# Narrower moving operands for the value product and the router product of a one-core hybrid attention and mixture-of-experts layer

## Chip, core and metric

The program runs on one NeuronCore of a Trainium2 chip. The metric is the device time of one execution in microseconds (us). Its engines are TensorE (PE in the rows, with its weight loads listed apart as PEld), VectorE (DVE), ScalarE (ACT), GpSimd (POOL) and SyncE (SP), which here issues most of the DMA transfers. On TensorE a product has a stationary operand, which is loaded by an instruction LDWEIGHTS, and a moving operand, whose columns are then streamed by MATMUL.

## What is computed

One layer over 1024 prompt tokens and 8 x 16 sample tokens. Of the reference, the change touches two products, the last line of the sparse attention and the two router products of the mixture of experts:

```python
    p = jax.nn.softmax(logits, axis=-1).astype(v.dtype)
    return jnp.einsum('bqhn,bqnhd->bqhd', p, v_sel)            # 8 heads of 64 columns
...
    g_logits = (x @ w_router_group + b_router_group).astype(jnp.float32)      # 4 columns
...
    e_logits = (x @ w_router_expert + b_router_expert).astype(jnp.float32)    # 16 columns
```

All inputs are float32. Around these lie a combined input projection, an indexer that picks 256 keys for each query, a recurrent branch, an output projection with a layer norm, and 16 experts.

## The kernel before

The kernel is written engine by engine; the order on each engine is the order of its code, and semaphores tie the engines together. Two kinds of product occur. `mm3` (lines 492 to 494) splits float32 operands into a high and a low part of type fp32r and makes three products. `mm` of two plain float32 tiles becomes two pairs of LDWEIGHTS and MATMUL in the trace: two passes over the same columns. `tr` is a product with the identity that transposes; it is one pair.

**Attention over the prompt.** Tokens lie in 8 query tiles of 128, each with 8 heads. PE runs a loop over i = 0 to 66, with query tile t = i // 8 and head h = i % 8. An iteration issues, in this order, the logits of head i (line 1054: stationary the padded queries, moving 128(t+1) key columns), the value product of head i - 3 (line 1066: stationary a block of 128 x 128 of the transposed probabilities `PT`, moving columns of `V`, t+1 blocks, so 2(t+1) passes) and the transposes of the probabilities of head i - 2 (line 1075). DVE takes the row maximum (line 1769), ACT the exponential (lines 1399 and 1400), and the two take turns, by odd and even head, to copy the transposed probabilities to `PT` (ACT line 1407, DVE line 1777). The value product of a head waits for this copy, the transposes wait for the exponential, and the logits wait for the row maximum of the head two before.

Before the change the value product streams the 128 columns of a pair of heads and leaves 128 columns in PSUM for each head; the 64 that belong to the head are read from there:

```python
v.tensor_tensor(ON[...], PS[:, 6 + hf, :].rearrange("p (k r c) -> p k r c", k=2, r=2)[:, :, r, HD * r:HD * r + HD], ...)
```

The whole loop has 288 such products (8 heads x 36 blocks), which are 576 passes.

**Router.** There are 9 token tiles. After the layer norm `turn_x1(t)` transposes a tile (line 1150, 8 pairs), ACT copies it to `X1T` (line 1547), and `router(t)` multiplies it with the router weights `RLG` (line 1161, 8 products, 16 passes). `RLG` has 128 columns, of which 20 are loaded by DMA; POOL clears it first (line 854), and SP waits for that before it loads the weights (line 697). The first routers are issued between the last products of the output projection, router(t - 4) after its token tile t and before turn_x1(t - 3); the last ones come behind it, each waiting for ACT's copy. DVE adds the bias (line 1911) and goes on to the choice of experts.

Three other places are used as rows below. Line 909 at the start transposes the input tokens (128 columns each). Line 936 is a single float32 product with a stationary block of 128 x 128 and 8 moving columns. Line 914 is a run of 8 transposes of 40 rows: 128 stationary columns, 40 moving ones.

Of the kernel before, what the change touches and what calls it, by code (L numbers as in the profile page):

```python
# [11 lines left out]
KB = D // 128  # L12
# [4 lines left out]
H, HD = 8, 64  # L17
# [42 lines left out]
def build(nc, I, O):  # L60
# [3 lines left out]
    def sb(name, shape, at, dt=f32):  # L64
        return nc.alloc_sbuf_tensor_at(name, shape, dt, offset=at)
# [50 lines left out]
    R2 = XLo + 36864  # L116
# [11 lines left out]
    V = sb("v", [128, TT, 512], R3)  # L128
# [39 lines left out]
    PT = sb("p_T", [128, 2, 1024], R6 + 18432 + 12288)  # L168
# [42 lines left out]
    WC = 256  # L211
    NWC = D // WC
    X1T = sb("x1_T", [128, 3, KB, 128], R2)
    RLG = sb("router", [128, KB, 128], R2 + 12288)
    LNP = sb("ln_params", [128, 4, D], M2)
    C0 = M2 + 16384

# [38 lines left out]
    PS = nc.alloc_psum_tensor("psum", [128, 8, 512], f32)  # L256
# [72 lines left out]
    s_block_products = sem("block_products")  # L329
# [45 lines left out]
    s_zero = sem("zero")  # L375
# [60 lines left out]
    blocks = []  # L436
# [129 lines left out]
    with nc.Block() as block:  # L566
# [3 lines left out]
        def _(sp):  # L570
# [123 lines left out]
                sp.dma_start(YACC[:, t, :], x_rows(t)).then_inc(s_xres[1], 16)  # L694
            sp.wait_ge(s_block_merged, 2 * KB)
            sp.dma_start(BEFORE[:, :], I["c_before"]).then_inc(s_lnp, 16)
            sp.wait_ge(s_zero, 2)
            with nc.allow_non_contiguous_dma(reason="router weights have short rows"):
                for c_, name, w in ((0, "w_router_group", 4), (4, "w_router_expert", 16)):
                    sp.dma_start(RLG[:, :, c_:c_ + w], I[name].rearrange("(k p) n -> p k n", p=128)).then_inc(s_lnp, 16)  # L700
# [12 lines left out]
                sp.dma_start(WD[e][:, :, :], WD_D[e]).then_inc(s_down_loaded[e], 16)  # L713
            sp.wait_ge(s_slot, 1)
            with sp.If(overflowing(sp)):
                sp.wait_ge(s_zero, 3)
                with sp.Fori(0, E) as e:
                    for j in range(MT_MAX - 1):
                        for h in range(2):
                            sp.dma_start(XS_N[bass.ds(e, 1), j][:, :, h, :].rearrange("o p d -> (o p) d"),  # L720
                                         XG[:, 0, 0, :]).then_inc(s_of, 16)
# [48 lines left out]
        def _(pool):  # L770
            g = nc.gpsimd
# [78 lines left out]
            pool.wait_ge(s_smp_out_turned, BATCH_S)  # L850
            for p_ in range(BA_0, NPIECE):
                split_piece(p_)
            pool.wait_ge(s_block_products, 3 * len(blocks))
            g.memset(RLG[:, :, :], 0.0).then_inc(s_zero, 1)
            pool.wait_ge(s_w_out_products, 1)
            for c in range(1, NWC):
                for q in range(2):
# [41 lines left out]
        def _(pe):  # L899
            mm, tr = nc.tensor.matmul, nc.tensor.transpose  # L900
            pe.wait_ge(s_misc, 16)
            for t in range(TT):
                for hf in range(2):
# [4 lines left out]
                    for k in range(4):  # L908
                        last = tr(PS[:, i % 4, 128 * k:128 * k + 128],
                                  XIN[:, t % 3, 128 * (4 * hf + k):128 * (4 * hf + k) + 128], IDENT)  # L910
                    last.then_inc(s_x_transposed, 1)
            pe.wait_ge(s_const, 16 * 10)
            for k in range(KB):
                last = tr(PS[:, 4, NV * k:NV * k + NV], VIN[0:NV, 128 * k:128 * k + 128], IDENT[0:NV, 0:NV])
# [45 lines left out]
            for c, (name, c0, w) in enumerate(CHUNKS):  # L960
                for t in range(TT):
# [19 lines left out]
                    if name == "kw":  # L981
                        last = tr(PS[:, gi % 4, 0:KW], KWT[:, ts], IDENT[0:KW, 0:KW])
# [62 lines left out]
            for i in range(TP * H + 3):  # L1045
                if i < TP * H:
                    t, h = divmod(i, H)
                    hp, n = h // 2, 128 * (t + 1)
                    if h == 0:
                        pe.wait_ge(s_queries_padded, t + 1)  # L1050
                    wait(pe, s_max_done, i - 1)
                    for k0 in range(0, n, 512):
                        m = min(512, n - k0)
                        last = mm(PS[:, 2 * (i % 2) + k0 // 512, 0:m], QZ[t % 2][:, h, :], KT[:, hp, k0:k0 + m],  # L1054
                                  start=True, stop=True)
                    last.then_inc(s_logits, 1)
                if i >= 3:
                    a = i - 3
                    t, h = divmod(a, H)
                    if h == 0 and t >= 1:  # L1060
                        turn_out(t - 1)
                    if h == H // 2:
                        wait(pe, s_attn_lo, t)
                    pe.wait_ge(s_p_T_stored[a % 2], a // 2 + 1)
                    for k in range(t + 1):
                        last = mm(PS[:, 6 + h // 4, 128 * (h % 4):128 * (h % 4) + 128], PT[:, a % 2, 128 * k:128 * k + 128],  # L1066
                                  V[:, k, 128 * (h // 2):128 * (h // 2) + 128], start=k == 0, stop=k == t)
                    last.then_inc(s_values_added, 1)
                if 2 <= i < TP * H + 2:
                    a = i - 2  # L1070
                    t = a // H
                    pe.wait_ge(s_exp_done, a + 1)
                    wait(pe, s_p_T_stored[(a - 1) % 2], (a + 1) // 2)
                    for k in range(t + 1):
                        last = tr(PS[:, 4 + k // 4, 128 * (k % 4):128 * (k % 4) + 128],  # L1075
                                  P[:, a % 3, 128 * k:128 * k + 128], IDENT)
                    last.then_inc(s_p_turned, 1)
# [75 lines left out]
            def router(t):  # L1153

                pe.wait_ge(s_x1t, 2 * t + 2)
                wait(pe, s_logits_ready, t - 1)
                if t == 0:
                    pe.wait_ge(s_states_rows, 2)
                    pe.wait_ge(s_lnp, 16 * 7)
                for k in range(KB):  # L1160
                    last = mm(PS[:, 6 + t % 2, 0:128], X1T[:, t % 3, k, :], RLG[:, k, :], start=k == 0, stop=k == KB - 1)
                last.then_inc(s_logit_products, 1)

            for c in range(NWC):
# [864 lines left out]
```

## Time and profile before

| | |
|---|---|
| median of 3 runs | 1838.76 us (1838.23 to 1840.95) |
| profiled execution, span | 1838.4 us, 0.36 us below the median |
| PE busy | 1607.0 us (87%), 9886 pairs of load and product |
| DVE, ACT, POOL busy | 825.6, 537.5, 441.6 us |
| chain that ended last | PE 66%, DVE 22% |

The span runs from the first to the last instruction of the profiled execution, and the table's shares are shares of it. Nothing beyond the span is listed for that execution, so its own time is taken as the span. A matmul's duration includes the time in which its last columns run through the array; the next one starts before that, so the distance between two starts, not the duration, is what a product costs in a row of products.

### The profile page before, as it was taken

To read this page: it belongs to the slowest core of one execution; us is meant where nothing else is said; L and a number is where in the kernel's file an instruction comes from. 1 tells how busy PE (TensorE), PEld (TensorE's weight loads), DVE (VectorE), ACT (ScalarE), POOL (GpSimd) and SP (SyncE) were. 2 spreads that over 40 slices of the span, in tenths; PEclk is the share of its full clock that TensorE was granted. 3 is DMA by queue.
4 is the path that set the end of the run, shared out by engine and by line. 5 is a ranking of instruction groups with operands and counts; after the bars stand their busy time and mean duration, and the time that the engine had idled before them with its cause. 6 is when DMAs were issued, how large, how long until landed. Compare 5 with 4: busy or idle time off the path is not lost.

```text
span 1838.4 us, 24783 instructions
## 1 busy us (share of the span) xinstructions
PE 1607.0 (87%) x9886; PEld 1409.3 (77%) x9886; DVE 825.6 (45%) x1555; ACT 537.5 (29%) x1056; POOL 441.6 (24%) x482
## 2 busy tenths in 40 slices
PE   6988899999589988899999989999993499999920
PEld 5944699999567776799899889999993377777710
DVE  4048399999944443224455541114264011211117
ACT  4256222111155433204656530003111121111025
POOL 2700297422100000133343332332201200000045
PEclk8989999999899999999999999999997699999965
DMA  5100111222550007431111111116005687877645
GB/s 172 33 7 1 52 36 59 63 91 83 158 167 1 24 1 252 154 113 38 47 32 46 44 29 47 41 41 226 27 1 191 212 260 229 261 252 233 195 133 193
DMA packets 135785, 195.16 MB, mean 106 GB/s; under 512 B 14644, under 2 KB 88884, under 8 KB 135680
## 3 DMA queue, kind: packets, MB, share of 16 engines
q1 hardware_dynamic: 130496, 174.83, 30.2%
q0 software_dynamic: 5184, 18.88, 3.0%
q8 instruction: 72, 1.18, 0.3%
q14 instruction: 33, 0.27, 0.0%
HBM read 144.48 MB, written 49.20 MB: 105 GB/s over the span
## 4 chain that ended last, share of the span: by engine, by line
PE 66%; DVE 22%; DMA 3%; POOL 3%; ACT 3%; issue 2%; SPq 0%; POOLq 0%; DVEq 0%; ACTq 0%
PE psum L492 11%; PE psum L493 11%; PE psum L494 11%; PE psum L1209 9%; PE psum L1230 6%; DVE compare_out L1731 5%; DVE psum L1731 5%; PE psum L1066 4%; PE psum L1054 3%; PE psum L1028 2%; PE psum L1075 2%; PE psum L932 2%; DVE scores L1692 1%; PE psum L1201 1%; PE psum L1126 1%
## 5 line engine op out<-in xcount | busy, mean ns | idle before, releaser
L492 PE MATMUL psum<-x_hi,ring_hi 128*128 128x384 f32 x768 | 259.2, 337 | 0.5 <-ACT v L1366 0.5
L493 PE MATMUL psum<-x_hi,ring_lo 128*128 128x384 f32 x768 | 256.7, 334 | 0.0
L494 PE MATMUL psum<-x_lo,ring_hi 128*128 128x384 f32 x768 | 256.7, 334 | 0.0
L822 POOL CAST ring_hi<-ring_raw 128x512 fp32r<-128x512 f32 x88 | 65.0, 738 | 566.8 <-PE psum L494 394.8
L1209 PEld LDWEIGHTS psum<-expert_rows_T,w_gate_up 128*128 128x128 f32 x1024 | 169.1, 192 | 8.5 <-issue 8.5
L492 PE MATMUL psum<-w_hi,x_hi 128*128 128x256 f32 x576 | 169.3, 294 | 5.0 <-DVE channel_vectors L1637 3.7
L1209 PE MATMUL psum<-expert_rows_T,w_gate_up 128*128 128x192 f32 x1024 | 171.0, 329 | 0.7 <-ACT expert_rows_T L1562 0.7
L493 PE MATMUL psum<-w_hi,x_lo 128*128 128x256 f32 x576 | 164.7, 286 | 0.0
L494 PE MATMUL psum<-w_lo,x_hi 128*128 128x256 f32 x576 | 164.5, 286 | 0.0
L492 PEld LDWEIGHTS psum<-x_hi,ring_hi 128*128 128x128 f32 x768 | 144.2, 188 | 1.7 <-ACT v L1366 0.7
L493 PEld LDWEIGHTS psum<-x_hi,ring_lo 128*128 128x128 f32 x768 | 144.2, 188 | 1.1
L494 PEld LDWEIGHTS psum<-x_lo,ring_hi 128*128 128x128 f32 x768 | 144.2, 188 | 0.0
L823 POOL TENSOR_TENSOR ring_lo<-ring_raw,ring_hi 128x512 fp32r<-128x512 f32 x88 | 129.3, 1469 | 7.0
L492 PEld LDWEIGHTS psum<-w_hi,x_hi 128*128 128x128 f32 x576 | 112.2, 195 | 5.3 <-issue 3.8
L1230 PE MATMUL psum<-w_down,expert_hidden 128*96 128x512 f32 x256 | 112.6, 593 | 0.8 <-issue 0.8
L1731 DVE TENSOR_SCALAR_CACHE_REDUCE compare_out<-scores,candidate_bits 128x640 bf16<-128x640 f32 (+2 forms) x128 | 112.1, 876 | 1.1
L493 PEld LDWEIGHTS psum<-w_hi,x_lo 128*128 128x128 f32 x576 | 112.4, 195 | 0.0
L494 PEld LDWEIGHTS psum<-w_lo,x_hi 128*128 128x128 f32 x576 | 112.2, 195 | 0.0
L883 POOL DMA_INDIRECT gathered_expert_out<-y_by_expert,slot x18 | 24.1, 1341 | 333.1 <-issue 333.1
L1956 DVE TENSOR_TENSOR expert_hidden<-psum,expert_silu 128x384 f32<-128x384 f32 x16 | 8.9, 558 | 198.0 <-PE psum L1209 198.0
L1731 DVE TENSOR_SCALAR_CACHE_REDUCE psum<-scores,candidate_bits 128x512 f32<-128x512 f32 (+2 forms) x96 | 97.6, 1016 | 0.0
L1066 PEld LDWEIGHTS psum<-v,p_T 128*128 128x128 f32 x576 | 71.3, 194 | 29.4 <-DVE p_T L1777 12.8
(322 smaller groups left out, 3200.4 us busy)
## 6 DMA issues: line engine op xcount, KB each, us to landing
w_gate_up<-in_w_gate_up SPq DMA_DIRECT2D x16, 2048.0 KB, 8.9
ring_raw<-in_w_in SPq DMA_DIRECT2D x64, 256.0 KB, 3.0
w_down<-in_w_down SPq DMA_DIRECT2D x16, 1024.0 KB, 6.3
x_by_expert<-zeros SPq DMA_DIRECT2D x32, 384.0 KB, 5.2
expert_rows<-x_by_expert SPq DMA_DIRECT2D x16, 768.0 KB, 11.0
y_by_expert<-expert_out SPq DMA_DIRECT2D x16, 768.0 KB, 7.4
w_raw<-in_w_in SPq DMA_DIRECT2D x16, 512.0 KB, 4.5
k_cache<-in_cache_k SPq DMA_DIRECT2D x8, 1024.0 KB, 8.1
```

Of the source, the lines that this page charges most:

```text
L492: nc.tensor.matmul(out, ah, bh, start=first, stop=False)
L493: nc.tensor.matmul(out, al, bh, start=False, stop=False)
L494: return nc.tensor.matmul(out, ah, bl, start=False, stop=last)
L822: link(g.tensor_copy(RHI[:, p_ % 2, :, :], RRAW[:, p_ % 2, :, :]))
L823: g.tensor_tensor(RLO[:, p_ % 2, :, :], RRAW[:, p_ % 2, :, :], RHI[:, p_ % 2, :, :].bitcast(f32), ALU.subtract).then_inc(s_piece_split, 1)
L932: mm(PS[:, 4 + d % 4, 0:n], QIT[:, h // 2, 128 * t:128 * t + 128], (KIZ if h % 2 else KIT)[:, k0:k0 + n], start=True, stop=True).then_inc( ...
L1028: mm(PS[:, 6 + j % 2, 0:RC], WRG[:, gt, :], XC[:, RC * c:RC * c + RC], start=True, stop=True).then_inc(s_lru_gate_products, 1)
L1054: last = mm(PS[:, 2 * (i % 2) + k0 // 512, 0:m], QZ[t % 2][:, h, :], KT[:, hp, k0:k0 + m], start=True, stop=True)
L1066: last = mm(PS[:, 6 + h // 4, 128 * (h % 4):128 * (h % 4) + 128], PT[:, a % 2, 128 * k:128 * k + 128], V[:, k, 128 * (h // 2):128 * (h // ...
L1209: last = mm(PS[:, bank + m // 2, MS * (m % 2):MS * (m % 2) + MS], wg[:, k, 128 * m:128 * m + 128], xgt[:, k, :], start=k == 0, stop=k == K ...
L1230: last = mm(PS[0:MR, 6 + j % 2, :], HE[:, par, k, MR * h:MR * h + MR], WD[par][:, k, 512 * nn:512 * nn + 512], start=k == 0, stop=k == 1)
L1731: v.tensor_scalar(out[:, 0:n], SC[:, o_:o_ + n], CAND[:, j:j + 1].bitcast(f32), c0_, ALU.is_ge, ALU.add, accum_out=CNT[:, j:j + 1]).then_i ...
```

## The change

`V` is indexed by the head's own 64 columns, which are written to the place in PSUM that DVE already reads; `RLG` has 20 columns; the clearing of `RLG` and SP's wait for it are gone, and the count of the one later wait on that semaphore is one lower.

```diff
-    RLG = sb("router", [128, KB, 128], R2 + 12288)
+    RLG = sb("router", [128, KB, 20], R2 + 12288)
...
             sp.dma_start(BEFORE[:, :], I["c_before"]).then_inc(s_lnp, 16)
-            sp.wait_ge(s_zero, 2)
             with nc.allow_non_contiguous_dma(reason="router weights have short rows"):
...
-                sp.wait_ge(s_zero, 3)
+                sp.wait_ge(s_zero, 2)
...
-            pool.wait_ge(s_block_products, 3 * len(blocks))
-            g.memset(RLG[:, :, :], 0.0).then_inc(s_zero, 1)
...
                     for k in range(t + 1):
-                        last = mm(PS[:, 6 + h // 4, 128 * (h % 4):128 * (h % 4) + 128], PT[:, a % 2, 128 * k:128 * k + 128],
-                                  V[:, k, 128 * (h // 2):128 * (h // 2) + 128], start=k == 0, stop=k == t)
+                        o0 = 128 * (h % 4) + HD * (h % 2)
+                        last = mm(PS[:, 6 + h // 4, o0:o0 + HD], PT[:, a % 2, 128 * k:128 * k + 128],
+                                  V[:, k, HD * h:HD * h + HD], start=k == 0, stop=k == t)
...
-                    last = mm(PS[:, 6 + t % 2, 0:128], X1T[:, t % 3, k, :], RLG[:, k, :], start=k == 0, stop=k == KB - 1)
+                    last = mm(PS[:, 6 + t % 2, 0:20], X1T[:, t % 3, k, :], RLG[:, k, :], start=k == 0, stop=k == KB - 1)
```

No instruction changes its place on any engine: PE has as many rows as before. PE in the second query tile of the attention, before (a float32 product stands in one row here, for both of its passes; the last number is the output's columns):

```order
L1066 MATMUL psum<-v,p_T 128x128 [waits p_T_stored_0]
L1066 MATMUL psum<-v,p_T 128x128
L1075 MATMUL psum<-misc,p 128x128 [waits p_T_stored_0,exp_done]
L1075 MATMUL psum<-misc,p 128x128
L1054 MATMUL psum<-k_T,q_padded_111 128x256 [waits max_done]
```

The same place on PE after the change, where the file is three lines shorter above it:

```order
L1064 MATMUL psum<-v,p_T 128x64 [waits p_T_stored_0]
L1064 MATMUL psum<-v,p_T 128x64
L1073 MATMUL psum<-misc,p 128x128 [waits p_T_stored_0,exp_done]
L1073 MATMUL psum<-misc,p 128x128
L1051 MATMUL psum<-k_T,q_padded_111 128x256 [waits max_done]
```

Only the output's columns differ; the waits and the neighbours are the same.

## Rows read from the trace of the kernel before

**Rows 1.** The page: span, and the chain that ended last, by engine and line.

```profile
span 1838.4 us, 24783 instructions
...
PE 66%; DVE 22%; DMA 3%; POOL 3%; ACT 3%; issue 2%; SPq 0%; POOLq 0%; DVEq 0%; ACTq 0%
PE psum L492 11%; PE psum L493 11%; PE psum L494 11%; PE psum L1209 9%; PE psum L1230 6%; DVE compare_out L1731 5%; DVE psum L1731 5%; PE psum L1066 4%; PE psum L1054 3%; PE psum L1028 2%; PE psum L1075 2%; PE psum L932 2%; DVE scores L1692 1%; PE psum L1201 1%; PE psum L1126 1%
```

**Rows 2.** Busy us (instructions) of PE, PEld, DVE, ACT, POOL, then PEclk, DMA share, GB/s.

```profile
518.00:597.00 79.00, 74.86 (x464) 55.45 (x463) 40.08 (x113) 42.78 (x122) 4.88 (x8) 1.00 0.18 52
597.00:677.00 80.00, 79.15 (x513) 62.25 (x511) 37.66 (x64) 37.46 (x75) 1.22 (x2) 1.00 0.04 14
```

**Rows 3.** Timeline, 660 to 667 us: start, length of the run, instruction, count.

```profile
660.20 1.95 PE L1066 MATMUL psum<-v,p_T 128*128 128x128 f32 x16
...
664.58 1.95 PE L1066 MATMUL psum<-v,p_T 128*128 128x128 f32 x16
664.58 1.75 PEld L1066 LDWEIGHTS psum<-v,p_T 128*128 128x128 f32 x15 [0.24 <-issue]
666.36 0.93 PE L1075 MATMUL psum<-misc,p 128*128 128x128 f32 x7
```

**Rows 4.** Timeline around lines 936 and 914.

```profile
181.09 0.30 PEld L936 LDWEIGHTS psum<-misc,wi_spread 128*128 128x128 f32 x2 [3.72 <-issue]
181.20 0.19 PEld L936 LDWEIGHTS psum<-misc,wi_spread 128*128 128x128 f32 x1
181.12 0.36 PE L936 MATMUL psum<-misc,wi_spread 128*128 128x8 f32 x2 [2.92 <-DVE wi_spread L1698]
27.20 0.57 PEld L914 LDWEIGHTS psum<-misc,vectors_in 40*128 40x128 f32 x8 [0.17 <-issue]
```

**Rows 5.** Groups by line and shape: count, busy us, mean ns of one.

```profile
L1066 PE MATMUL psum<-v,p_T 128*128 128x128 f32 x576 | 79.9, 284 | 8.3 <-ACT p_T L1407 5.3 <-DVE p_T L1777 2.6
L1054 PE MATMUL psum<-k_T,q_padded 128*128 128x512 f32 x96 | 47.8, 593 | 0.0
```

**Rows 6.** Who PE waited for, 518 to 597 us, then 504 to 518 us.

```profile
PE psum L1066 <- ACT p_T L1407: 3.0, 8, 0.7
...
PE psum L1054 <- DVE row_max L1769: 18.1, 1, 18.1
```

**Rows 7.** The last routers: timeline, and busy time of that stretch.

```profile
1389.81 2.05 PE L1161 MATMUL psum<-router,x_T 128*128 128x128 f32 x16 [0.74 <-ACT x_T L1547]
1393.47 2.05 PE L1161 MATMUL psum<-router,x_T 128*128 128x128 f32 x16 [0.74 <-ACT x_T L1547]
...
1385.00:1399.00 14.00, 10.61 (x88) 9.93 (x88) 4.10 (x9) 4.90 (x8) 0.00 (x0) 1.00 1.04 397
```

**Rows 8.** The same columns by stretch (second row: line 909 alone); then a timeline.

```profile
16.20:26.40 10.20, 5.81 (x26) 5.41 (x27) 4.35 (x7) 4.49 (x8) 0.00 (x0) 0.50 0.70 249
16.20:26.40 10.20, 5.81 (x26) 5.41 (x27) 0.50 0.70 249
26.40:29.80 3.40, 1.49 (x16) 1.20 (x14) 3.14 (x5) 1.29 (x3) 0.00 (x0) 0.99 0.00 0
504.50:514.50 10.00, 8.17 (x29) 6.61 (x30) 2.46 (x15) 6.92 (x28) 0.89 (x2) 0.50 0.99 289
514.50:527.00 12.50, 10.04 (x61) 7.07 (x61) 6.32 (x26) 7.44 (x29) 1.24 (x3) 1.00 0.95 272
1402.00:1449.00 47.00, 1.56 (x6) 1.46 (x6) 9.34 (x42) 0.21 (x1) 17.36 (x18) 0.50 0.60 224
...
510.25 0.42 PE L1054 MATMUL psum<-k_T,q_padded 128*128 128x128 f32 x1
511.41 0.64 PE L1054 MATMUL psum<-k_T,q_padded 128*128 128x128 f32 x2
```

**Rows 9.** The clearing on POOL, and SP's load of the router weights.

```profile
1262.82 0.95 POOL L854 MEMSET router<- 128x1024 f32 x1 [10.42 <-PE psum L494]
1269.13 0.43 SPq L700 DMA_DIRECT2D router<-in_w_router_group  x1
```

## Prediction

> **What bounds the kernel now.** I read the page first. The span is 1838.4 us, and the chain that ended last lies on PE for 66% of it, of which line 1066, the value product, holds 4% [rows 1]: some 70 us in which work can be saved, if the product gets shorter. Then the attention by stretch: from 597 us on (query tiles 5 to 7) PE is busy for 79.15 of 80.00 us, so there each nanosecond of PE counts; from 518 to 597 us (tiles 1 to 4) it is busy for 74.86 of 79.00, and DVE and ACT for half of the time [rows 2]. In those tiles the value product still waits now and then for ACT's copy of the probabilities (3.0 us in 8 waits), and in tile 0 PE waits for the row maximum (18.1 us in one wait) [rows 6].
>
> So the question is what a value product costs, load and stream. In a row of 16 passes the starts of 16 products span 1.95 us less one duration; the mean duration is 0.284 us [rows 3, 5], so a pass takes (1.95 - 0.28) / 15 = 0.111 us. The 15 loads tell the same: 1.75 us less one load of 0.19, over 14, is 0.111 us [rows 3, 4].
>
> What would the stream alone need? The duration grows from 284 ns at 128 columns to 593 at 512 [rows 5], that is 309 / 384 = 0.80 ns a column, 0.10 us for 128 columns and 0.05 for 64. What would the load alone need? Line 936 shows it: stationary 128 x 128 as here, but only 8 moving columns. Its first load starts at 181.09, its second at 181.20 [rows 4]. With almost nothing to stream, the next pass still comes 0.11 us later. Loads of float32 blocks of 128 columns follow each other at 0.11 us, whatever is streamed between.
>
> **The change, part by part.**
>
> *Value product, within a run.* 576 passes, each from 0.10 us of streaming to 0.05. By line 936 the load of 0.11 us takes the place of the stream, so a pass stays at 0.11 us: 0. The bounds: nothing, and 4 ns a pass (0.111 down to 0.107, the lower edge of the rounded 0.11), on the 512 passes that are followed by another of their run, 2.0 us. I take nothing.
>
> *Value product, at the end of a run.* The last pass of a run is followed by a transposing product of line 1075, whose load is shorter: the eight loads of line 914, also with 128 stationary columns, span 0.57 us, at most 0.07 us apiece, and since that includes all of the last load, I take 0.06 [rows 4]. Today the last pass streams 0.11 us before the transposes can stream; then it needs 0.05, and the short load 0.06. That saves 0.11 - 0.06 = 0.05 us in each of the 64 runs, one per head. In tiles 5 to 7 all of it counts: 24 x 0.05 = 1.2 us. In tiles 1 to 4 the heads are copied in turn by ACT and DVE, and the copy that waits behind an exponential or a row maximum hides part; I take half, 32 x 0.05 / 2 = 0.8 us (bounds 0 and 1.6). In tile 0 PE waits for the row maximum anyway: 0 (at most 8 x 0.05 = 0.4). Together 2.0 us, between 1.2 and 3.2.
>
> *Router.* The same, nine runs of 16 passes: 16 products in 2.05 us, less a first load and one duration, is again 0.11 a pass [rows 7]. Of 20 columns the stream is 0.02 us, the load still 0.11. After eight of the runs come the transposes of line 1150, 8 x 0.05 = 0.4 us; the last one's result comes 108 x 0.8 ns = 0.09 us earlier. All are in line: the last routers wait for ACT's copy [rows 7], which waits for the transposes of line 1150, which stand behind the router before on PE. Together 0.5 us, at most another 135 x 4 ns = 0.5 us.
>
> *Clearing and wait.* The 0.95 us on POOL end at 1263.77 us, SP issues the router weights at 1269.13 [rows 9], 5.4 us later: SP was held by its earlier transfers, not by the clearing. The transfers keep their number of pieces. If SP came to that place before POOL, the wait would have cost up to 0.95 us, and its removal would give that back; the late routers come 120 us later [rows 7], so the price is 0 either way.
>
> *Readers.* DVE reads the same 64 columns of PSUM as before. Nothing is added on another engine.
>
> Sum: 2.0 + 0.5 = 2.5 us off 1838.4, 1835.9 us. The median of the runs is 0.36 us above the profiled execution, so I forecast 1836.3.
>
> The Trainium skill's page "TensorE: Matmul & The Clock Gate" has rules for both answers. Its section on the back-to-back gap gives N / 2.4 + 2.5 ns for an isolated warm product, by which 64 columns fewer would give an estimated 27 ns for each of 576 passes, 15 us in all. Its section on LDWEIGHTS says that a load takes about P / 1.2 ns for P columns whatever else is in it, an estimate of 107 ns for 128, and by that rule the change would give almost nothing. The rows of line 936 side with the second.
>
> **The rivals.**
>
> *The stream sets the pace after all* (a load is fetched further ahead in a long run than line 936 with its two passes can show). Then a pass falls to about 0.055 us. Tiles 5 to 7 have 336 passes, 18.8 us; tiles 1 to 4 have 224, of which half counts, 6.3 us; the router's 144 passes fall from 0.11 to some 0.03, 12 us. Together 37 us, 1801 us. Against it: the loads of line 1066 do not run ahead of their products; fifteen of them take 0.111 us each [rows 3].
>
> *The upper bound of every term.* All 64 ends of runs (3.2 us), 4 ns on each pass (2.0 and 0.5), and the router's 0.5: 6.2 us, 1832.2, as a median 1832.6.
>
> *The clock.* The change takes columns from PE and leaves its pace. The granted clock shows what that can do: at the start of the attention it stays at 0.50 (1.2 GHz) for 10 us in which PE is busy for 8.17, and goes to 1.00 (2.4 GHz) only then; behind the routers it is at 0.50 for 47 us in which PE is busy for 1.56 [rows 8]. If the last routers, with 20 columns in place of 128, no longer look busy, the clock falls there and not behind them. At the lower clock two passes of 128 columns are 0.64 - 0.42 = 0.22 us apart [rows 8], twice as far. A round of router and transposes, 3.66 us from 1389.81 to 1393.47 [rows 7], would be longer by 16 x 0.11 and 8 x 0.11 us (a transpose, too, costs 0.11 at the higher clock, (0.93 - 0.28) / 6 in [rows 3]), 2.6 us. One round outweighs the gain; a fall at about 1388 us, behind the first late router, costs two rounds, a last router (1.8) and a set of transposes (0.9), 7.9 us: 1838.4 - 2.5 + 7.9 = 1843.8, as a median 1844.2. The time is longer than before by more than 0.2% once 2.4 rounds are hit. A later rise at the start of the attention is the same mechanism: each head of tile 1 (4 passes of value, 2 transposes, 2 passes of 256 columns) would cost up to 4 x 0.11 + 2 x 0.11 + 2 x 0.21 = 1.1 us more. For it: the stretch of the last routers keeps 10.61 busy us of 14.00 [rows 7] only as long as a pass that streams little counts. Against it: the transposes stay, and between 16.2 and 26.4 us PE ran nothing but the 26 transposes of line 909, and the clock rose from 0.50 to 0.99 behind them [rows 8]; and at the attention the runs of logits stay.
>
> If transposes did not count for the clock, the fall would be all but certain, since beside them the late routers stream almost nothing. The Trainium skill's page "TensorE: Matmul & The Clock Gate" says in its part on transposes that they do not count as busy in the same way. The trace disagrees: the rise to 0.99 at 26.4 us had only transposes before it.
>
> *No effect at all* (the ends of runs hidden too): 1838.8; it lies 2.5 us from the forecast and inside its own range.
>
> **How the numbers follow.** A measurement of this kernel tells about 0.2% (3.7 us) from no change, so faster means below 1835.1, slower above 1842.4. The forecast, loads that set the pace and a clock as before, with its own range 1834 to 1839: 0.63, of which 0.06 is below 1835.1. The upper bounds, 1832.5 to 1834.5: 0.12. The stream: 0.05. The clock: 0.20, between 1837 and 1845, 0.12 of it above 1842.4. Faster 0.06 + 0.12 + 0.05 = 0.23, slower 0.12, same 0.65. The range 1832.5 to 1842.5 leaves out the stream (0.05) and the worse half of the clock (0.12).
>
> **What would show it.** In the profile after, line 1066's counterpart: runs of 16 loads still 0.11 us apart while the duration of a product falls from 284 to about 230 ns; the first transposing product 0.06 us behind the last value product; 4.38 us per head in tile 7 (660.20 to 664.58, [rows 3]) become 4.33. The router's rounds 3.61 in place of 3.66. PEclk 1.00 until the routers end, and its rise in the attention within a few us of 10 us behind its start. The forecast is wrong if the loads follow each other faster than 0.10 us, or if the clock falls before 1395 us.

## The result, and the profile after

The changed kernel took 1851.71 us (median of 4 runs, 1846.45 to 1854.21), the kernel before 1839.64 us (4 runs): ratio 1.0062, 95% interval 1.0046 to 1.0078. It is slower by 8 to 14 us, where 2.5 us less was forecast. The profiled execution of the changed kernel took 1851.48 us and has a span of 1849.7 us, so 1.8 us lie outside a span; the comparisons below are of spans and of starts within them.

The page of the changed kernel, its span and the granted clock in 40 slices:

```profile
span 1849.7 us, 24775 instructions
...
PEclk8989899999799998999999999999995699999965
```

The chain that ended last is as in [rows 1], on PE for 66%, with the value product (now line 1064) at 3% in place of 4%. One slice of the clock row stands out: the 31st (1387 to 1434 us) shows 5. To find the 11.3 us, take the start of the same instruction in both traces at the borders of the stages. PE's timeline of the kernel before, then of the changed kernel (the rows are the first logits, the last value product, the first value product of the sample tokens, the first two routers and the last one, the experts' first transposes):

```profile
485.53 0.71 PE L1054 MATMUL psum<-k_T,q_padded 128*128 128x128 f32 x4 [0.58 <-ACT sigmoid_out L1389]
685.75 2.05 PE L1066 MATMUL psum<-v,p_T 128*128 128x128 f32 x16 [1.32 <-DVE p_T L1777]
707.04 1.07 PE L1126 MATMUL psum<-v_cache,p_sample_T 128*32 128x128 f32 x10
1359.60 2.05 PE L1161 MATMUL psum<-router,x_T 128*128 128x128 f32 x16 [0.72 <-ACT x_T L1547]
1365.24 1.95 PE L1161 MATMUL psum<-router,x_T 128*128 128x128 f32 x16
1397.14 2.05 PE L1161 MATMUL psum<-router,x_T 128*128 128x128 f32 x16 [0.74 <-ACT x_T L1547]
1449.06 3.06 PE L1201 MATMUL psum<-misc,expert_rows 96*128 96x96 f32 x16 [37.67 <-DMA expert_rows<-x_by_expert]
```

```profile
486.12 0.71 PE L1051 MATMUL psum<-k_T,q_padded 128*128 128x128 f32 x4 [0.58 <-ACT sigmoid_out L1387]
684.38 2.00 PE L1064 MATMUL psum<-v,p_T 128*128 128x64 f32 x16 [1.31 <-DVE p_T L1775]
708.45 1.07 PE L1124 MATMUL psum<-v_cache,p_sample_T 128*32 128x128 f32 x10
1360.98 2.24 PE L1159 MATMUL psum<-router,x_T 128*128 128x20 f32 x16 [0.72 <-ACT x_T L1545]
1368.16 1.86 PE L1159 MATMUL psum<-router,x_T 128*128 128x20 f32 x16
1394.22 3.60 PE L1159 MATMUL psum<-router,x_T 128*128 128x20 f32 x16 [0.69 <-ACT x_T L1545]
1400.28 3.60 PE L1159 MATMUL psum<-router,x_T 128*128 128x20 f32 x16 [0.69 <-ACT x_T L1545]
1406.35 3.60 PE L1159 MATMUL psum<-router,x_T 128*128 128x20 f32 x16 [0.69 <-ACT x_T L1545]
1460.01 3.05 PE L1199 MATMUL psum<-misc,expert_rows 96*128 96x96 f32 x16 [37.85 <-DMA expert_rows<-x_by_expert]
```

| stage, from start to start | before | after | difference |
|---|---|---|---|
| span's start to first logits | 485.53 | 486.12 | +0.59 |
| first logits to last value product | 200.22 | 198.26 | -1.96 |
| from there to the sample tokens' first value product | 21.29 | 24.07 | +2.78 |
| from there to first router | 652.56 | 652.53 | -0.03 |
| first router to last router | 37.54 | 45.37 | +7.83 |
| last router to the experts' transposes | 51.92 | 53.66 | +1.74 |
| from there to the span's end | 389.34 | 389.69 | +0.35 |

The attention gave what was forecast, 2.0 us. From the first value product of a tile to that of the next, tiles 1 to 4 are 0.83 us shorter and tiles 5 to 7 0.93. The other 0.19 lie in tile 0 and are not shown to be the change's: tile 0 took 11.85 us before, 11.66 after and 11.27 in run 2 below, whose value product is that of before and whose clock rose at 510 us in place of 514.5.

The rest was lost behind the attention, above all in the routers and what follows them. But each column of the table is one execution, and not every difference in it comes back in another. The late routers' does: from router 5 (counted from 0) to the experts' transposes it is 62.88 us before, 71.05 after and 70.89 in run 2, which has the narrow router too. The first router's does not: its start to the second's is 5.64 us before and 7.18 after, and 5.59 in run 2 with the same 20 columns. Nor does that of the stage behind the attention: beside 21.29 before and 24.07 after stand 23.53, 23.59 and 23.70 us in runs 2, 6 and 9, whose value product is that of before, and 21.47 in run 1, which has the narrow one. So some 4 us of the 11.3 are not shown to come from the change.

The same columns as [rows 2], for the changed kernel:

```profile
597.00:677.00 80.00, 78.68 (x515) 61.57 (x514) 38.06 (x64) 36.98 (x75) 1.22 (x2) 1.00 0.05 14
687.00:700.00 13.00, 10.24 (x45) 7.58 (x50) 3.99 (x8) 2.98 (x5) 0.00 (x0) 0.50 0.77 268
1385.00:1389.80 4.80, 3.26 (x30) 3.05 (x29) 4.66 (x9) 1.38 (x3) 0.00 (x0) 1.00 0.77 230
1389.80:1406.00 16.20, 14.49 (x66) 13.29 (x65) 2.17 (x6) 3.28 (x6) 0.00 (x0) 0.50 0.84 321
```

Read the granted clock, the seventh figure. Behind the attention it is at 0.50 (1.2 GHz) from 687 us on, where the kernel before fell at 695.4. In the late routers it falls at 1389.8 and stays at 0.50, although PE is busy for 14.49 of 16.20 us; before, the whole stretch ran at 1.00 [rows 7]. Ahead of the fall the busy times don't differ: PE is busy for 3.26 of the 4.80 us up to 1389.8, and before for 3.30 of the 4.80 us at the same place (1382.22 to 1387.02), both at 1.00. At 0.50 a router takes 3.60 us in place of 2.05, and a round, 1394.22 to 1400.28 and on to 1406.35, takes 6.06 in place of 3.66.

That the loads' pace itself did not change is seen in tile 7, PE's timeline of the changed kernel where the clock is at 1.00, with a piece of the loads' timeline:

```profile
659.12 1.89 PE L1064 MATMUL psum<-v,p_T 128*128 128x64 f32 x16
660.85 1.04 PE L1073 MATMUL psum<-misc,p 128*128 128x128 f32 x8
661.73 1.88 PE L1051 MATMUL psum<-k_T,q_padded 128*128 128x512 f32 x4
663.45 1.89 PE L1064 MATMUL psum<-v,p_T 128*128 128x64 f32 x16
...
663.45 0.64 PEld L1064 LDWEIGHTS psum<-v,p_T 128*128 128x128 f32 x5 [0.23 <-issue]
```

Five loads in 0.64 us, less one of 0.19, are still (0.64 - 0.19) / 4 = 0.11 us apart. The run of 16 is 1.89 long in place of 1.95 [rows 3], the transposes follow at 1.73, that is 0.06 behind the last pass's start (15 x 0.111 = 1.67), and a head takes 663.45 - 659.12 = 4.33 us in place of 4.38.

### The profile page after: what moved, and what is told of

Its sections match the earlier page's. It is cut to its first block, busy times and chain, and to the rows that moved or that the text cites. A ratio compares the mean times of both kernels' runs of the same rounds, so it can differ in the third digit from the quotient of the medians.

```text
span 1849.7 us, 24775 instructions
## 1 busy us (share of the span) xinstructions
PE 1617.7 (87%) x9879; PEld 1418.6 (77%) x9886; DVE 824.4 (45%) x1555; ACT 537.9 (29%) x1056; POOL 440.4 (24%) x481
## 4 chain that ended last, share of the span: by engine, by line
PE 66%; DVE 22%; DMA 3%; POOL 3%; ACT 3%; issue 2%; SPq 0%; POOLq 0%; DVEq 0%; ACTq 0%
PE psum L492 11%; PE psum L493 11%; PE psum L494 11%; PE psum L1207 9%; PE psum L1228 6%; DVE compare_out L1729 5%; DVE psum L1729 5%; PE psum L1064 3%; PE psum L1051 3%; PE psum L1025 2%; PE psum L929 2%; PE psum L1073 2%; PE psum L1199 1%; PE psum L1124 1%; DVE scores L1690 1%
```

## The experiments

The theory after the result: the loads set the pace of both products, and what was lost was lost by the granted clock, because PE streams fewer columns there and not because it is busy for less time. The rivals are named at each run. A profile shows one execution, and they differ ahead of the edits too: the attention's first value product starts at 507.84 us before and 508.42 after, but at 500.85, 504.83 and 503.89 in runs 3, 4 and 5, where PE waits less for the first row maximum (11.85 us in run 5, 18.08 before). So spans are compared by stage. Runs 1 to 4 were compared with the kernel before at 1838.65 us (30 executions), runs 5 to 8 at 1839.48 (34).

**1. The value product alone** (the diff's value part on the kernel before).

> Only the value product is narrow; the router keeps 128 columns, its clearing and its wait. Theory (fewer streamed columns let the clock fall): 2.0 us gained in the attention, about 2 lost again behind it because the clock falls at about 687 us as in the changed kernel; at the router PEclk stays 1.00 until about 1400. Time within 1.5 us of the kernel before. Rival (the clock falls at the router for another reason, such as an earlier attention): the late routers run at 0.50 here too, 8 us longer than before.

Measured: 1838.19 us (12 runs), ratio 1.0004 (0.9985 to 1.0022). First logits to last value product: 483.69 to 681.96, 198.27 us, the same 1.95 us less than before. The clock stayed at 1.00 in all routers and fell at 684.7 us. So this part alone is not what made the kernel slower; nor does its 2 us show in the median. That 2 us would be lost again behind the attention did not come out of the profile, although the clock fell there as expected. The last value product and the first value product of the sample tokens, in this run and then in run 2, which has 128 columns there:

```profile
681.96 2.00 PE L1067 MATMUL psum<-v,p_T 128*128 128x64 f32 x16 [1.32 <-DVE p_T L1778]
703.43 1.07 PE L1127 MATMUL psum<-v_cache,p_sample_T 128*32 128x128 f32 x10
...
682.65 2.05 PE L1063 MATMUL psum<-v,p_T 128*128 128x128 f32 x16 [1.31 <-DVE p_T L1774]
706.18 1.07 PE L1123 MATMUL psum<-v_cache,p_sample_T 128*32 128x128 f32 x10
```

That is 21.47 us here, with the fall at 684.7, and 23.53 in run 2, with the fall at 691.2.

**2. The router alone** (the changed kernel with the value product of before).

> Only the router is narrow (and its clearing and wait are gone); the value product keeps 128 columns. Theory (fewer streamed columns): the attention and the clock behind it are as before (1.00 until about 695 us), the late routers run at 0.50: 8 to 10 us slower than the kernel before. Rival (the router's columns are not the cause): within 1 us of the kernel before.

Measured: 1848.93 us (7 runs), ratio 1.0046 (1.0028 to 1.0065). Its late routers by stretch:

```profile
1387.50:1403.00 15.50, 14.13 (x65) 12.97 (x64) 2.00 (x6) 2.98 (x5) 0.00 (x0) 0.50 0.87 330
```

The last two routers in PE's timeline of this run:

```profile
1397.67 3.60 PE L1158 MATMUL psum<-router,x_T 128*128 128x20 f32 x16 [0.69 <-ACT x_T L1544]
1403.74 3.60 PE L1158 MATMUL psum<-router,x_T 128*128 128x20 f32 x16 [0.69 <-ACT x_T L1544]
```

Rounds of 6.07 us at 0.50, as in the changed kernel. The router's part of the change is enough, and most of the loss comes from it. It is the 108 columns fewer together with the clearing and the wait that are gone; run 8 lacks these two as well and keeps its clock, so their absence alone does not lower it. At the first router the clock held here.

**3. The changed kernel with one added product ahead of the first router and of each of routers 5 to 8.** The added product's result is not used:

```diff
+            def fill(done):
+                pe.wait_ge(s_mix_added, done)
+                mm(PS[:, 0, 0:256], IDENT, MISC[:, 0:256], start=True, stop=True)
...
             for t in range(TT - 3, TT):
+                fill(TT * NWC - 3)
                 router(t - 1)
                 turn_x1(t)
+            fill(TT * NWC - 3)
             router(TT - 1)
```

> The changed kernel with work added: one product of the identity with 256 columns of constants, two passes, in the pause before the first router and before each of the last four, into a PSUM bank that nothing reads any more. Theory (PE streams too little there): PEclk stays 1.00 until the routers end, the 8 us of the late routers and the 1.3 us at the first come back, about 1842.5 us, although PE has more to do. Rival (the clock falls for another reason): the clock falls as before, and the added products cost 0 to 4 us: 1852 to 1856.

Measured: 1843.13 us (12 runs), ratio 1.0020 (1.0003 to 1.0037): 4.5 us above the kernel before, where the changed kernel was 12.1 above it, with more work on PE. But not as meant. The clock held at the first router, as it did in run 2 without an added product, and fell at 1384.8 us all the same, for 13.6 us:

```profile
1384.80:1398.40 13.60, 13.60 (x59) 12.01 (x57) 0.59 (x5) 3.56 (x6) 0.00 (x0) 0.50 0.89 338
```

PE is busy for all of 13.60 us here at the half clock, with its passes mostly of 20 columns; behind this stretch the clock rose again. One product a round did not hold the clock. From router 5 to the experts' transposes the profile still loses 5.4 us of the 8.2 (68.32 us), and the clock was at 0.50 from 671.4 us in the attention's last heads as well. That the time of the profiled execution (1843.12 us) came out near the expected 1842.5 is luck: its first value product starts 7 us earlier than before, which the edit doesn't touch.

**4. The changed kernel with a router of 64 columns** (`RLG` of 64 columns, cleared and waited for as before).

```diff
-                    last = mm(PS[:, 6 + t % 2, 0:20], X1T[:, t % 3, k, :], RLG[:, k, :], start=k == 0, stop=k == KB - 1)
+                    last = mm(PS[:, 6 + t % 2, 0:64], X1T[:, t % 3, k, :], RLG[:, k, :], start=k == 0, stop=k == KB - 1)
```

> The changed kernel with a router of 64 columns, 20 loaded and 44 cleared, clearing and wait put back: the load of a pass still sets its pace. Theory (what counts is how many columns are streamed): a router run streams 16 x 0.05 us and not 16 x 0.02, beside its transposes that is enough, the clock stays 1.00 to the end of the routers, about 1842 us. Rival (a product that is shorter than its load does not count at all for the clock): the clock falls as with 20 columns, about 1852 us.

Measured: 1842.98 us (12 runs, 1835.9 to 1856.5), ratio 1.0033 (1.0010 to 1.0056). Here are the late routers and the end of the attention by stretch:

```profile
1386.00:1401.00 15.00, 11.25 (x96) 10.33 (x94) 5.22 (x10) 5.62 (x9) 0.00 (x0) 1.00 1.02 384
...
674.00:684.60 10.60, 8.22 (x38) 7.42 (x37) 1.22 (x1) 1.02 (x1) 0.00 (x0) 0.50 0.00 0
```

The last two value products of the attention in PE's timeline of this run:

```profile
677.95 3.67 PE L1067 MATMUL psum<-v,p_T 128*128 128x64 f32 x16 [1.11 <-ACT p_T L1408]
684.65 3.68 PE L1067 MATMUL psum<-v,p_T 128*128 128x64 f32 x16 [1.31 <-DVE p_T L1778]
```

With 64 columns and the same loads the clock stays at 1.00 in the late routers, and nothing is lost there: 62.56 us from router 5 to the experts' transposes, 62.88 before. With 20 columns it fell. Busy time does not tell the two apart: it was the same ahead of the fall (above), and the 14.49 of 16.20 us behind it are high since every pass takes longer at 0.50. Part of the loss that is left lies in the last heads of the attention, which have no logits beside them: the clock fell there at 674.0 us, and two runs of value products took 3.7 us in place of 2.00. Tile 7 took 3.8 us more than in the changed kernel (33.41 and 29.59, from its first value product to its last); in run 3, with the same narrow value product, it took 32.73, and in run 1 29.59.

**5. The value product at 128 columns in tile 7 alone, at 64 in tiles 0 to 6; the router as before.**

```diff
-                        last = mm(PS[:, 6 + h // 4, 128 * (h % 4):128 * (h % 4) + 128], PT[:, a % 2, 128 * k:128 * k + 128],
-                                  V[:, k, 128 * (h // 2):128 * (h // 2) + 128], start=k == 0, stop=k == t)
+                        o0, c0, w = 128 * (h % 4), 128 * (h // 2), 128
+                        if a < TP * H - 8:
+                            o0, c0, w = o0 + HD * (h % 2), HD * h, HD
+                        last = mm(PS[:, 6 + h // 4, o0:o0 + w], PT[:, a % 2, 128 * k:128 * k + 128],
+                                  V[:, k, c0:c0 + w], start=k == 0, stop=k == t)
```

> The kernel before with the value product at 64 columns in query tiles 0 to 6 and at 128 in tile 7; the router as before. Theory (the clock falls where fewer columns are streamed, and the ends of runs give 0.05 us a head): granted clock 1.00 from the early attention to the end of tile 7, no fall ahead of 695 us as in the kernel before; the gain of tiles 1 to 6, about 24 heads' worth of 0.05 us, stays: 1.2 us below before, that is 1837.4, and in the aligned traces a gap of -1 to -2 us that is still there at 735 us. Rival (the fall behind the attention of the changed kernel has nothing to do with the columns of the value product): the clock is at 0.50 within 670 to 695 us here too, and the gap at 735 us is 0 or above: 1838.6 or more.

Measured: 1838.18 us (12 runs), ratio 0.9989 (0.9977 to 1.0002). A gain of the expected size is within the interval, and so is none. The marks, put in absolute times, don't decide: the clock fell at 690.0 us, inside the rival's 670 to 695, but the attention ended 5.5 us earlier than before, 4.0 of them ahead of the first value product, where nothing was edited. Counted from the end of the last value product, the fall came 7.7 us behind it, as before (7.6). Tiles 1 to 6 took 134.72 us in place of 136.13, so their gain is there. The end of the attention by stretch:

```profile
670.00:683.50 13.50, 8.54 (x71) 7.64 (x69) 3.54 (x7) 1.76 (x3) 0.00 (x0) 1.00 0.00 0
```

Over all profiles the fall nearest to the attention's end came, with 64 columns in tile 7, at 686.7 (changed kernel), 684.7, 671.4 and 674.0 us (runs 1, 3, 4), that is less than 1 us behind the end of the last value product, or, in runs 3 and 4, some 13 and 14 us ahead of it; with 128 columns there, in the kernel before and runs 2 and 5 to 9, at 695.4, 691.2, 690.0, 691.5, 694.4, 692.6 and 691.9, some 6 to 9 us behind that end. So the width of tile 7 moves the fall. It cost time where the fall came ahead of the end, 3.1 and 3.8 us in tile 7 of runs 3 and 4; that a fall just behind the end costs any is not shown (run 1).

**6. The kernel before with added products in two long waits of PE** (36 in the wait for the first row maximum, 80 in the wait for the experts' rows).

```diff
+                    if i == 2:
+                        for _ in range(36):
+                            mm(PS[:, 5, 0:256], IDENT, MISC[:, 0:256], start=True, stop=True)
                     wait(pe, s_max_done, i - 1)
...
+            for _ in range(80):
+                mm(PS[:, 0, 0:256], IDENT, MISC[:, 0:256], start=True, stop=True)
             pe.wait_ge(s_slot, 1)
```

> The kernel before, products unchanged, with products added that compute nothing that is used: 36 (72 passes of 256 columns) while PE waits 18.1 us for the first row maximum, and 80 (160 passes) while it waits 37.7 us for the experts' rows. Theory (what the half clock costs is given back if PE streams columns in its waits): granted clock 1.00 in the attention's first tile and in the first expert's products, which before run at 0.50 until 514.5 and 1456.6 us. A head of tile 0 takes 1.4 us at 0.50 and would take about 1.0, 7 heads, 2 to 3 us; the 7.6 us behind 1449 shrink by about 3: together 5 us, 1833.6. Rival (those stretches are paced by ACT, DVE or DMA and not by PE's clock): within 1 us of before, 1838.6, or above it by the products that outlast the wait.

Measured: 1838.72 us (11 runs), ratio 0.9994 (0.9985 to 1.0002). The clock by stretch:

```profile
486.00:503.80 17.80, 14.02 (x65) 11.87 (x63) 16.03 (x30) 1.64 (x3) 0.00 (x0) 1.00 0.97 280
503.80:510.60 6.80, 5.91 (x22) 4.88 (x23) 1.78 (x10) 4.27 (x21) 0.00 (x0) 0.50 0.92 261
...
1415.10:1452.70 37.60, 34.72 (x169) 30.15 (x168) 0.00 (x0) 2.23 (x5) 17.36 (x18) 1.00 0.82 293
1452.70:1456.10 3.40, 3.40 (x13) 3.40 (x12) 0.00 (x0) 0.80 (x1) 0.00 (x0) 0.50 0.00 0
```

The products raised the clock in the waits or held it, but ended some 2 us before the waits did, and the clock fell within 3 us or so of the start of the work. Whether it fell for that pause or for the work behind it, the run does not tell. The 5 us were not reached, and the run does not settle what a clock at 1.00 throughout would give.

**7. The same with the value product of run 5.**

> The added products of the run with filled waits and, besides, the value product at 64 columns in tiles 0 to 6. Theory: 1.2 us less than that run, about 1832.4; the clock stays at 1.00 in the attention, since with it high from the start there is no late rise to lose. Rival (the narrow product costs clock somewhere in the early tiles, where PE waits for ACT and DVE): a stretch at 0.50 between 515 and 650 us and a time above that of the run with filled waits.

Measured: 1838.91 us (11 runs), ratio 0.9991 (0.9978 to 1.0004), the same as run 6. The clock was at 0.50 from 503.4 to 516.9 us here, at the attention's start, which reaches 2 us into the rival's 515 to 650, and from there to 694.4 at 1.00, so tiles 1 to 6 cost no clock once it was up; the 1.2 us less were not seen in the median.

**8. The changed kernel with two added products ahead of the first router and of routers 4 to 8, and the value product at 128 columns in tile 7.** The edits are those of runs 3 and 5, with two products in `fill` and one more call.

> The changed kernel (router 20 columns) with the value product at 128 columns in tile 7 alone and two added products (4 passes of 256 columns, 0.86 us at the full clock) ahead of the first router and of each of routers 4 to 8, where PE waits 0.7 us for ACT's copy in any case. Theory (all that was lost was lost by the clock): granted clock 1.00 until the last router's end, no fall ahead of 695 us; the added products outlast the waits by at most 0.2 us a round, 1 us in all: the changed kernel's time less its 11 to 12 us of lost clock, plus 1: about 1839.5. Rival (the narrow router loses by something else, or the clock falls for lack of columns in any case): 1845 or more, with the late routers at 0.50 for over half of their time.

Measured: 1836.51 us (10 runs), ratio 0.9985 (0.9975 to 0.9996): 3.0 us below the kernel before, where the changed kernel was 12.1 above it, and 3 us less than expected. The late routers by stretch:

```profile
1384.00:1398.00 14.00, 12.12 (x96) 11.05 (x95) 3.53 (x13) 4.77 (x8) 0.00 (x0) 1.00 0.98 375
```

The last two rounds in PE's timeline of this run (line 1168 is the added products):

```profile
1389.64 1.03 PE L1168 MATMUL psum<-misc 128*128 128x256 f32 x4
1390.55 1.96 PE L1161 MATMUL psum<-router,x_T 128*128 128x20 f32 x16
...
1393.26 1.03 PE L1168 MATMUL psum<-misc 128*128 128x256 f32 x4
1394.16 1.96 PE L1161 MATMUL psum<-router,x_T 128*128 128x20 f32 x16
```

The clock is at 1.00 to the end, the added products lie where PE waited for ACT's copy, and a round takes 1394.16 - 1390.55 = 3.61 us. The same 20 columns that cost 8 us in the changed kernel cost nothing here; the only difference in these rounds is the products added in the wait, which fill it with loads and columns alike. That columns alone do it is seen in run 4, where the router's loads and PE's waits are those of the changed kernel.

**9. Passes by size.** In the kernel before, nine groups of 8 float32 products in the wait for the experts' rows, with `w` stationary and `m` moving columns:

```diff
+            def probe(w, m, n):
+                for _ in range(n):
+                    mm(PS[0:w, 0, 0:m], IDENT[:, 0:w], MISC[:, 0:m], start=True, stop=True)
+            probe(128, 256, 16)
+            for w in (128, 64, 32):
+                for m in (20, 64, 128):
+                    probe(w, m, 8)
+                    probe(128, 256, 3)
             pe.wait_ge(s_slot, 1)
```

> The kernel before with products added that compute nothing that is used, in PE's wait of 37.7 us for the experts' rows: nine groups of 8 float32 products (16 passes) with 128, 64 or 32 stationary columns by 20, 64 or 128 moving ones, each followed by three products of 128 x 256 that keep the clock at 1.00. Theory (a pass takes the longer of its load and its stream, the load by the stationary columns): 128 stationary columns give 0.11 us a pass at 20, 64 and 128 moving columns; 64 give about 0.06 at 20 and 64 and 0.11 (or the stream's 0.10) at 128; 32 give about 0.03 at 20, 0.05 at 64 and 0.10 at 128. Rival (a float32 pass has a fixed cost of 0.11 us, or a load does not depend on its columns): 0.11 us a pass in all nine. Time: within 1 us of before, if the clock at the experts' start is of no weight, as in the run with filled waits.

One execution: 1841.58 us beside 1838.29, from which nothing is read. The granted clock was 1.00 from 1415.6 to 1449.4 us, around all nine groups. The groups by shape (stationary rows x columns, moving rows x columns, count, busy us, mean ns):

```profile
L1237 PE MATMUL psum<-misc 128*64 128x128 f32 x16 | 2.0, 276 | 0.0
L1237 PE MATMUL psum<-misc 128*128 128x128 f32 x16 | 1.9, 275 | 0.0
L1237 PE MATMUL psum<-misc 128*32 128x128 f32 x16 | 1.9, 274 | 0.0
L1237 PE MATMUL psum<-misc 128*128 128x64 f32 x16 | 1.9, 272 | 0.0
L1237 PE MATMUL psum<-misc 128*128 128x20 f32 x16 | 1.9, 261 | 0.0
L1237 PE MATMUL psum<-misc 128*64 128x64 f32 x16 | 1.1, 225 | 0.0
L1237 PE MATMUL psum<-misc 128*64 128x20 f32 x16 | 1.1, 214 | 0.0
L1237 PE MATMUL psum<-misc 128*32 128x64 f32 x16 | 1.1, 220 | 0.0
L1237 PE MATMUL psum<-misc 128*32 128x20 f32 x16 | 0.7, 187 | 0.0
```

Busy time less one duration, over 15, is the pass: 128 stationary columns give (1.9 - 0.27) / 15 = 0.11 us at 20, 64 and 128 moving columns; 64 by 64 and 64 by 20 give 0.06, 32 by 64 also 0.06, 32 by 20 gives 0.03, and any stationary width gives 0.11 at 128 moving columns. A pass takes the longer of its load and its stream, and the rival of a fixed cost is out. The Trainium skill's page "TensorE: Matmul & The Clock Gate", in its section on LDWEIGHTS, says that a load takes about P / 1.2 ns for P columns, an estimate of 107 and 53 ns for 128 and 64; these rows agree (0.11 and 0.06 us).

## Why the prediction was wrong

- **Value product, within a run: 0.** Right. The loads stayed 0.11 us apart, and run 9 shows the rule behind line 936: with 128 columns to load, nothing is gained below 128 columns to stream.
- **Value product, at the ends of runs: 2.0 us, between 1.2 and 3.2.** Right: 1.96 us from the first logits to the last value product in the changed kernel, 1.95 in run 1; 0.05 us a head in tile 7. Of the parts, tiles 5 to 7 gave 0.93 in place of 1.2 and tiles 1 to 4 0.83 in place of 0.8; 0.19 lie in tile 0 and are not shown to be the change's. The bound of 4 ns a pass is a slip, since a rounded 0.11 reaches down to 0.105 and not 0.107; nothing was taken for it.
- **Router: 0.5 us.** Right where the clock holds: rounds of 3.61 in place of 3.66 us in run 8, and of 3.61 to 3.62 in run 4 with 64 columns. In the changed kernel the term was buried.
- **Clearing and wait: 0.** No row of after contradicts it; no run priced it apart.
- **"A clock as before", the forecast's own condition with 0.63.** This step failed: the sum has no term for the clock. It was a rival with 0.20, at one place: a fall at about 1388 us for 7.9 us. It fell at 1389.8 us, and from router 5 (before 1386.18, after 1388.96, +2.78) to the experts' transposes (+10.95) it cost 8.2 us, and 8.0 in run 2: place and size of the rival were right, and its chance was not. Two more parts of the span's 11.3 us, 1.5 at the first router and 2.8 behind the attention, were not foreseen either; other executions don't repeat them (above), so their cause stays open.
- **Why its chance was put too low.** The argument against it was "the transposes stay", since behind transposes alone the clock had risen at 26.4 us [rows 8]. That row is right but does not carry over: 16 of the 24 passes in a late round are the router's, those fell from 128 columns to 20, and the transposes that stayed did not hold the clock. The argument for it went by busy time, 10.61 of 14.00 us, which did not differ ahead of the fall. At the attention "the runs of logits stay" was too broad: the last three value products (677.47, 681.51 and 685.75 us in the kernel before) have no logits beside them and wait for their copies, and they lie behind the stretch of [rows 2], which ends at 677.
- **The own time.** The profiled execution's span was taken for its time, and 1.8 us lie outside a span. The forecast, a median less 2.5 us, is not touched by it.
- **The rival that the stream sets the pace, 1801 us:** out, by the same rows of run 9.
- **The marks.** The fall of PEclk before 1395 us was named as what would make the forecast wrong, and it was. One mark was a poor one: the mean duration of a value product did not fall to 230 ns:

```profile
L1064 PE MATMUL psum<-v,p_T 128*128 128x64 f32 x576 | 76.5, 278 | 8.7 <-ACT p_T L1405 5.7 <-DVE p_T L1775 2.6
```

  It contains products at the half clock. And at the full clock the duration goes with the stationary columns too: at 64 moving ones it is 272 ns with 128 stationary and 225 with 64 (run 9), as if it held the wait for the load. A run of 16 is 0.06 us shorter, 1.89 in place of 1.95.

**What stays open.** Why the clock fell so much earlier against the attention's end in runs 3 and 4 than in run 1, with the same value product. It varies from execution to execution: of run 4's twelve, the seven up to 1843.6 us have a mean granted clock of 0.934 to 0.941, the five from 1848.5 us on 0.926 to 0.933. One profile of each run cannot show where in the others it fell. And that run 8's 3 us below before are the attention's 1.6 (484.71 to 683.31 is 198.60 us, against 200.22) and the router's half microsecond is argued from its rows, since the interval, 0.7 to 4.6 us, doesn't tell them apart from the scatter of the stages ahead.

## What to carry to other kernels

A float32 pass takes the longer of its load (by stationary columns) and its stream (by moving columns), so cutting moving columns below the stationary ones saves only at the ends of runs; both must shrink. Columns that cost no time may still be what holds the clock, as the router's did here (the changed kernel against run 4): before cutting them, look for the stretches where PE waits or only transposes beside them (here the last heads of a loop and a chain of router rounds), and ask what would still be streamed there. If columns are cut anyway, useless products in waits that exist can hold the clock at no cost in time (run 8). They lasted there until the next work started; one a round was not enough in run 3, and in run 6, where they ended 2 us early, the clock fell all the same, though why there is only argued.

## What was not expected of the hardware

PE busy for 13.60 of 13.60 us (run 3) and 14.49 of 16.20 (changed kernel) stayed at a granted clock of 0.50, while 11.25 of 15.00 (run 4) stayed at 1.00, with the same loads for the router in all; the moving columns of the router product were 20, 20 and 64. The cost of one lost stretch is large beside what is saved: a router round at 0.50 takes 6.06 us in place of 3.66. And removing useless columns made the kernel 12 us slower than before, while useless products added to the result of that, with the last tile's value product wide again, brought it 3 us below.
